# A decoder layer with a retrieval mixer on one core: the residual is kept in the result, and two of the last stores become accumulating DMAs

## The reference

```
    x = x + concat(attn, conv) @ w_out
    h = rms(x) ; q = h @ w_q ; the 16 best of 128*128 experts per head, by two sets of 128 keys
    ug = take(u, experts) ; vg = take(v, experts)              # (tokens, 128, 2048)
    act = gelu(einsum("tkd,td->tk", ug, h)) * gates
    x = x + einsum("tk,tkd->td", act, vg)
```

## Time and profile before

| | us |
|---|---|
| median of 3 runs | 2934.63 (2933.8 to 2936.33) |
| the profiled execution | 2936.09 |
| its span | 2934.0 |

### The profile page before, as it was taken

How to read it: one execution, slowest core, us unless ns; L and a number is a source line. 1 busy time by engine, 2 the same in 40 slices (tenths; PEclk the granted TensorE clock), 3 DMA queues, 4 the chain that set the end, 5 groups by cost and what they waited for, 6 DMA issues and landing times.

```text
span 2934.0 us, 40429 instructions
## 1 busy us (share of the span) xinstructions
PE 2875.9 (98%) x14769; PEld 2544.0 (87%) x14769; DVE 2391.8 (82%) x3106; ACT 1056.5 (36%) x1375; POOL 1667.4 (57%) x1078
## 2 busy tenths in 40 slices
PE   7999999999999999999999999999999999999999
PEld 6888778778899999999999999999997778877787
DVE  6555888855678898988989898899777989999898
ACT  4121333341333343434433343434233333333333
POOL 1000555500116667666766566577868888887762
PEclk9999999999999999999999999999999999999999
DMA  8998999979978998999999999999999999999999
GB/s 297 331 354 276 304 306 298 305 280 330 312 256 304 327 350 307 346 322 345 330 314 348 315 332 331 335 345 365 334 363 387 415 418 417 419 420 418 420 417 375
DMA packets 332718, 1010.00 MB, mean 344 GB/s; under 512 B 65748, under 2 KB 182496, under 8 KB 247072
## 3 DMA queue, kind: packets, MB, share of 16 engines
q1 hardware_dynamic: 181648, 523.28, 47.8%
q0 software_dynamic: 113344, 454.44, 42.7%
q10 hardware_dynamic: 37584, 30.43, 3.2%
HBM read 881.01 MB, written 127.01 MB: 344 GB/s over the span
## 4 chain that ended last, share of the span: by engine, by line
PE 56%; DVE 15%; POOL 10%; issue 8%; DMA 8%; ACT 1%; ACTq 0%; DVEq 0%; SPq 0%; POOLq 0%
PE ps L2021 18%; PE ps L2023 17%; PE ps L2022 17%; POOL dots L975 5%; DMA v_ring<-in_peer_v,experts 3%; DVE x_rows L1871 3%; POOL v_ring L986 3%; DVE u_row L1862 2%; DMA v_two<-in_peer_v 2%; PE ps L2262 2%; DVE x_one L1969 1%; DVE uT_lo L1830 1%; POOL grid L967 1%; DVE uT_lo L1835 1%; DVE v_lo L1920 1%
## 5 line engine op out<-in xcount | busy, mean ns | idle before, releaser
L2021 PE MATMUL ps<-hT_hi,uT_hi 128*128 128x384 f32 x2048 | 697.8, 341 | 6.8 <-DVE uT_lo L1835 2.6
L2023 PE MATMUL ps<-h2T_lo,uT_hi 128*128 128x384 f32 x2048 | 686.1, 335 | 0.0
L2022 PE MATMUL ps<-hT_hi,uT_lo 128*128 128x384 f32 x2048 | 684.9, 334 | 0.0
L967 POOL DMA_INDIRECT grid<-gates,grid_cells x256 | 541.7, 2116 | 80.3 <-issue 80.3
L2021 PE MATMUL ps<-v_hi,a_hi 128*128 128x512 f32 x1024 | 406.5, 397 | 26.0 <-DVE v_lo L1920 25.4
L2022 PE MATMUL ps<-v_hi,a_lo 128*128 128x512 f32 x1024 | 404.0, 395 | 0.0
L2023 PE MATMUL ps<-v_lo,a_hi 128*128 128x512 f32 x1024 | 403.8, 394 | 0.0
L1342 ACT ACTIVATE v_hi<-v_two 128x2048 fp32r<-128x2048 f32 x126 | 241.6, 1919 | 450.0 <-PE ps L2023 387.2
L2021 PEld LDWEIGHTS ps<-hT_hi,uT_hi 128*128 128x128 f32 x2048 | 384.6, 188 | 18.8 <-DVE uT_lo L1835 9.5
L2022 PEld LDWEIGHTS ps<-hT_hi,uT_lo 128*128 128x128 f32 x2048 | 384.9, 188 | 1.9
L2023 PEld LDWEIGHTS ps<-h2T_lo,uT_hi 128*128 128x128 f32 x2048 | 384.3, 188 | 0.0
(11 more groups left out here) (210 smaller groups left out, 4956.7 us busy)
## 6 DMA issues: line engine op xcount, KB each, us to landing
v_two<-in_peer_v SPq DMA_DIRECT2D x63, 2048.0 KB
u_tile<-uT_all SPq DMA_DIRECT2D x70, 1024.0 KB
u_tile<-in_peer_u SPq DMA_DIRECT2D x58, 1024.0 KB
grid_rows<-grid SPq DMA_DIRECT2D x32, 1024.0 KB
half_rows<-in_peer_u SPq DMA_DIRECT2D x58, 512.0 KB, 7.0
uT_all<-half_turned POOLq DMA_DIRECT2D x232, 128.0 KB, 5.0
near_rows<-in_peer_u SPq DMA_DIRECT2D x25, 1024.0 KB, 8.9
uT_all<-near_turned SPq DMA_DIRECT2D x100, 256.0 KB, 7.0
```

The source lines that it names most:

```text
L967: pool.indirect_dma_start(out=grid, out_offset=bass.IndirectOffsetOnAxis(ap=grid_cells[:, d, col:col + 1], axis=0), in_=gates[:, 2 + d, co ...
L2021: mm(out, a_hi, b_hi, start=first, stop=False)
L2022: mm(out, a_lo, b_hi, start=False, stop=False)
L2023: return mm(out, a_hi, b_lo, start=False, stop=last)
```

## The change

1. SP stores the residual of blocks 1 to 3 into the rows of the result itself, not into x_mid, which is gone.
2. x_one isn't loaded. The first of its 128 sums is a product (`tensor_scalar`), the others are as before. Behind the last of them POOL adds x_one onto block 1 of the result with an accumulating DMA (1 MB).
3. x_end for block 2 isn't loaded. DVE copies the four banks of block 2 out of PSUM, and POOL adds them onto block 2 of the result in two halves (512 KB each, behind the second and the fourth copy).
4. Block 3 is as before, with its residual loaded from the result.
5. SP ends behind its own stores and the three of POOL.

```diff
             for t in range(1, TB):
                 sp.wait_ge(out_added[t], OUT_CHUNKS)
-                sp.dma_start(x_mid[t - 1], x_rows[:, t, :]).then_inc(x_mid_stored, 16)
+                sp.dma_start(out_v[t], x_rows[:, t, :]).then_inc(x_mid_stored, 16)
...
             load_group(1, 1)
-            sp.dma_start(x_one[:, :], x_mid[0]).then_inc(x_in[1], 16)
...
-            for d in range(DENSE):
-                sp.dma_start(x_end[d][:, :], x_mid[1 + d]).then_inc(x_in[2 + d], 16)
+            sp.dma_start(x_end[1][:, :], out_v[3]).then_inc(x_in[3], 16)
             sp.dma_start(out_v[0], x_rows[:, 0, :]).then_inc(out_stored, 16)
-            sp.wait_ge(v_used, TILES)
-            sp.dma_start(out_v[1], x_one[:, :]).then_inc(out_stored, 16)
-            for d in range(DENSE):
-                for m in range(TB):
-                    cols = slice(m * CHUNK, (m + 1) * CHUNK)
-                    sp.wait_ge(x_end_ready, TB * d + m + 1)
-                    sp.dma_start(out_v[2 + d][:, cols], x_end[d][:, cols]).then_inc(out_stored, 16)
-            sp.wait_ge(out_stored, 16 * (2 + TB * DENSE))
+            for m in range(TB):
+                cols = slice(m * CHUNK, (m + 1) * CHUNK)
+                sp.wait_ge(x_end_ready, TB + m + 1)
+                sp.dma_start(out_v[3][:, cols], x_end[1][:, cols]).then_inc(out_stored, 16)
+            sp.wait_ge(out_stored, 16 * (1 + TB))
+            sp.wait_ge(sums_stored, 16 * 3)
...
+            pool.wait_ge(x_mid_stored, 16 * SWEPT_BLOCKS)
+            pool.wait_ge(v_used, TILES)
+            pool.dma_start(out_v[1], x_one[:, :], accum_op=ALU.add).then_inc(sums_stored, 16)
+            for half in range(2):
+                cols = slice(half * D // 2, (half + 1) * D // 2)
+                pool.wait_ge(x_end_ready, TB // 2 * (half + 1))
+                pool.dma_start(out_v[2][:, cols], x_end[0][:, cols], accum_op=ALU.add).then_inc(sums_stored, 16)
...
-                if c == 0:
-                    dve.wait_ge(x_in[1], 48)
...
+                if c == 0:
+                    v.tensor_scalar(x_one[:, :], v_ring[0][:, :], acts[:, 0:1], None, ALU.mult).then_inc(v_used, 1)
+                    return
...
-            for d in range(DENSE):
-                dve.wait_ge(x_in[2 + d], 48)
-                for m in range(TB):
-                    cols = slice(m * CHUNK, (m + 1) * CHUNK)
-                    dve.wait_ge(dense_done, TB * d + m + 1)
-                    v.tensor_tensor(x_end[d][:, cols], ps_dense[d][:, cols], x_end[d][:, cols], ALU.add)\
-                        .then_inc(x_end_ready, 1)
+            for m in range(TB):
+                cols = slice(m * CHUNK, (m + 1) * CHUNK)
+                dve.wait_ge(dense_done, m + 1)
+                v.tensor_copy(x_end[0][:, cols], ps_dense[0][:, cols]).then_inc(x_end_ready, 1)
+            dve.wait_ge(x_in[3], 48)
+            for m in range(TB):
+                cols = slice(m * CHUNK, (m + 1) * CHUNK)
+                dve.wait_ge(dense_done, TB + m + 1)
+                v.tensor_tensor(x_end[1][:, cols], ps_dense[1][:, cols], x_end[1][:, cols], ALU.add)\
+                    .then_inc(x_end_ready, 1)
```

More of the change, by code:

```diff
@@ L391, in decoder_layer @@
         mix_all = nc.dram_tensor("mix_all", (KT, P, SEQ), F32, kind="Internal").ap()
-        x_mid = nc.dram_tensor("x_mid", (SWEPT_BLOCKS, P, D), F32, kind="Internal").ap()
         ps = ctx.enter_context(nc.psum_tensor("ps", [P, 8, CHUNK], F32))
@@ L511, in decoder_layer @@
         out_stored = sem("out_stored")
+        sums_stored = sem("sums_stored")
         dve_step = sem("dve_step")
```

## The result

The changed kernel takes 2942.77 us (median of 22 runs, 2936.83 to 2948.88). The kernel before, on the same chip between the same runs, takes 2936.05 us (22 runs, 2933.39 to 2941.9). The ratio is 1.0022 with a 95% interval of 1.0016 to 1.0028, so the change costs 6.5 us (4.7 to 8.2): slower, by 0.22%, just more than the 0.2% that the prediction took for the least that a measurement can tell. The forecast was +3.5 us, no change. The base differs too: the prediction added to the 2934.63 us of three runs, and the median of 22 lies 1.4 us higher. So of the 4.7 us between 2938.1 and 2942.77, 1.4 are the base and 3.3 the effect.

What follows compares the result with a forecast made beforehand. PE (busy 193.15 of 200 us) and the DMA engines (share 1.01) were taken as nearly exhausted together in the last stage. Adding stores at the end +4.0, early gain -0.5: +3.5 us, 2938.1 us, range 2933.0 to 2942.5.

Steps and rivals of the forecast that it cites:

- Stores of blocks 1 to 3 into the result: SP's queue: three transfers of the same size at the same place, to the result instead of x_mid; cost 0.
- Copies and first sum: DVE: block 2's adds become PSUM copies, block 1's first sum a product without x_one as input; cost 0 each.
- The early gain: Start of last stage: without x_one's load v_two lands 2.5 us sooner; mostly handed back later, 0.5 us left.
- POOL's issue: End of kernel: an adding issue takes 1.16 us, starting at 2922.5 when the last sum is done.
- The case in which v_lo holds POOL's issue: DVE's v_lo, 2922.43 to 2924.71, delays POOL's issue: +5.7 us, 2940.3; chance 0.05.
- The rate of the addition: POOL's adding transfers at the end: twice the plain time, 5.0 us per MB, ratio read from small packets.
- The two other rates: Adding transfers at the plain rate, 2.5 us per MB (chance 0.23), or three passes, 7.5 us per MB (chance 0.18).
- the three-pass case: End of kernel: reading source, reading result and writing in turn, 7.5 us per MB; +8.5 us, 2943.1; chance 0.18.
- The work of the whole transfers: DMA engines at the end: 5.0 us for x_one and 5.0 for block 2's halves, then 2.8 for block 3's chunks.
- The begin, and the landing behind the last byte: Tail: first add moves from 2924.0, after the last sum at 2922.5; landing comes 0.8 us behind the last byte.
- The end of the program: Span's end: 0.4 us behind the last landing, as in the kernel before; landed 2937.6, end 2938.0.
- the load's neighbour stall: Sign: PE's stall ahead of the fifth tile near 2214 falls from 3.35 us to under 1 us.

Runs made afterwards that it cites:

- E1: Kernel before without the load of x_one, first sum a product, end as before; ratio to before 0.9996 (0.9987 to 1.0006).
- E5: Kernel before with the load of x_one moved behind the second v_two load on SP's queue; ratio to before 0.9996 (0.9985 to 1.0008).
- E3: Changed kernel with only block 2 added by POOL, block 1 loaded, summed and stored by SP as before; ratio to before 1.0030 (1.0020 to 1.0039).
- E6: Kernel before plus one 8-KB plain store to a scratch tensor as POOL's last act; ratio to before 1.0017 (1.0008 to 1.0026).
- before, again: Kernel before, unchanged, profiled a second time for scatter; stage 721.2 us, tail 11.4 us.
- E4: Changed kernel with POOL's three transfers as plain stores, no adding; ratio to before 1.0003 (0.9993 to 1.0012).
- E8: Changed kernel with x_one added once more, 1 MB onto an unused table, behind the first addition; ratio to before 1.0030 (1.0017 to 1.0042).
- after again: Changed kernel, unedited, profiled a second time for scatter; stage 721.5 us, tail 19.2 us.
- E2: Kernel before with only block 1 changed: x_one not loaded, POOL adds it, block 2 as before; ratio to before 1.0006 (0.9997 to 1.0016).
- E7: Changed kernel with block 2's two POOL transfers plain, block 1 still added; ratio to before 1.0010 (1.0001 to 1.0020).

## Why the prediction was wrong, point by point

**Stores of blocks 1 to 3 into the result: 0. Copies and first sum: 0.** Right. The four copies took 2.79 us, 0.70 each, next to 0.69 for the adds, and they began 3.3 us behind the last sum, as the adds had. DVE's end 8.84 us behind the last sum in both kernels says that neither the missing load of x_end nor the copies moved anything.

**The early gain: 2.5 us at its place, 0.5 left.** The end is right: 0.2 to 0.4 us in the stages, E1 not resolved, E5 handed back within the stage. The size at its place was too high. v_two is ready 1.6 us sooner, not 2.5, and PE's stall in the seven profiles without the load is 1.09 to 2.23 us (mean 1.8), not 0.9. With the load in its old place it is 3.35, 3.49 (E3), 3.24 (E6) and 1.94 (before, again), so the 3.35 of the earlier trace rows was an ordinary value and what was wrong is the 2.5: the time of 1 MB at the full rate was taken off v_two's landing whole. It did no harm, since nearly nothing of it was carried over; the forecast was lucky there.

**POOL's issue.** Its length was nearly right, its start was not: it began 0.6 us behind the last sum, not with it. The adding issue took 1.00 us beside v_lo (2918.28, with v_lo from 2917.61 to 2919.90), where the estimate was 1.16. The plain one of E4 took 0.61. The case in which v_lo holds POOL's issue is excluded. By the Trainium skill (GPSIMD Engine Reference, Specifications), GpSimd contends with VectorE's instructions that have two SBUF inputs. Here v_lo is such an instruction, and the two issues beside it show no hold; a hold is seen in the indirect issues of the earlier trace rows.

**The rate of the addition: twice the plain time.** The ratio holds for single packets in mid-transfer. After, in the 2 us from 2922, with nothing but additions of 8-KB packets in flight, and before, in the 2 us from 2924, with x_one's plain store:
```profile
q0 software_dynamic: 51, 0.42, 100.2%
```
```profile
q1 hardware_dynamic: 108, 0.78, 94.8%
```
51 packets in 1.002 x 2 x 16 = 32.1 engine-us are 629 ns each, at 209 GB/s:
```profile
2922.00:2924.00 2.00, 2.00 (x10) 1.61 (x9) 1.89 (x4) 0.00 (x0) 0.90 (x1) 1.00 1.00 209
```
That is half of the 418 of the earlier trace rows. On before's side 108 packets in 30.3 engine-us are 281 ns each; 13 of them are under 512 bytes (0.78 MB is 95 packets of 8 KB), and the other 95 would be 319 at most. So the ratio is near 2.0. The prediction had read it from packets of 4 bytes, and no row had shown that it would hold for 8 KB. The Trainium skill (Collectives: The Full Stack, The bandwidth ceiling) gives the adding step of a ReduceScatter two reads for each write, and half of AllGather's rate; at this size the trace agrees. The two other rates are excluded, by E8 above all. This deserves a warning: the measured 2942.77 us lies on the time of the three-pass case (2943.1), and a reader of the time alone would take that case for proven. Its 15 us of work for 2 MB are not there; the trace has 11.4 to 11.6.

**The work of the whole transfers: 10.0 us. First wrong term.** Twice the plain rate is right in mid-transfer and too low for the whole. 2 MB took 11.4 to 11.6 us, in after 5.8 for block 1 and 5.6 for block 2. In block 1's MB the first 16 packets, which make all 16 engines busy, take 1.29 us each, 0.66 more than later ones, and that is most of what it has over 5.0. Without such a beginning the price was right: E8's added MB took 5.1. Block 2's MB, in more and smaller packets, took 5.3 in E8, 5.6 and 5.9 in the profiles of after and 6.1 in E3, where the engines were idle before it. Block 3's chunks, with 2.8 us, were right. The sum of work is 14.3 us instead of 12.8: 1.5 us too low. Why the first packets take twice as long is open.

**The begin, and the landing behind the last byte: 1.5 and 0.8 us. Two more wrong sizes.** The data begin to move 2.15 us behind the last sum, not 1.5. The landing was put too high: from the end of the last packet to SP's release it is 0.35 to 0.4 us in both profiles of after. Between the two edges lie 15.5 us in after and 14.6 in after again, with 14.3 and 14.4 us of work in them. The rest, 1.2 and 0.2 us, was in no term: some engines are done before others. The windows of after's last us (columns as in the earlier trace rows) show a few engines still at work when the others have finished:
```profile
2932.00:2933.00 1.00, 0.00 (x0) 0.00 (x0) 0.00 (x0) 0.00 (x0) 0.00 (x0) 0.50 1.07 381
2933.00:2934.00 1.00, 0.00 (x0) 0.00 (x0) 0.00 (x0) 0.00 (x0) 0.00 (x0) 0.50 0.47 176
2934.00:2935.00 1.00, 0.00 (x0) 0.00 (x0) 0.00 (x0) 0.00 (x0) 0.00 (x0) 0.50 0.11 41
2935.00:2936.00 1.00, 0.00 (x0) 0.00 (x0) 0.00 (x0) 0.00 (x0) 0.00 (x0) 0.50 0.02 8
```
In before the share is 0.99 to the end of the stores. What makes single engines late here I could not settle. An addition and plain chunks stand in the same engines, and E8, with the same mixture, has no such thin end.

**The end of the program: 0.4 us behind the last landing. The step that failed.** I took the distance between the last landing and the span's end from before and carried it over to a program whose last transfers are POOL's. The DRAIN of POOL ends 3.1 to 3.2 us behind the landing of its last transfer in after, after again, E2, E4, E7 and E8, and 4.6 us behind it in E6 (2931.5 to 2936.1), and the program waits for it. In the kernel before, POOL's last transfer was a gather issued at 2904.8. Its last packet is at 2919.4 and the DRAIN ends at 2922.7, 3.3 us behind that packet (in after 3.4), so the same closing time stood in the profile of before, 11 us ahead of the end, where it cost nothing. SP's end to the span's end is 1.6 and 2.1 us now: 1.2 and 1.7 us too low. The prediction asked who waits for SP's last wait, but not what POOL itself does when it has nothing left.

The terms together, in us:

| term | predicted | after | after, again |
|---|---|---|---|
| last sum to the first packet | 1.5 | 2.15 | 2.15 |
| work of the engines | 12.8 | 14.3 | 14.4 |
| engines done unevenly | 0 | 1.2 | 0.2 |
| last packet to SP's release | 0.8 | 0.35 | 0.4 |
| SP's release to the span's end | 0.4 | 1.6 | 2.1 |
| tail | 15.5 | 19.6 | 19.2 |

The effect by the profiles, 7.8 to 8.2 less 0.2 to 0.4, is 7.4 to 8.0 us; the timed one is 6.5, with an interval of 4.7 to 8.2 that holds them.

**The cases.** The forecast's mechanism was right, its size too small by 3.0 us. The range, 2933.0 to 2942.5, missed the time by 0.3 us; the base, 1.4 us higher, is more than that. The slower side of the forecast rested nearly all on the case of three passes (0.18 of 0.22), which is excluded. What happened instead was no case: the work (1.5 us), the end of the program (1.2 to 1.7) and the begin (0.65) were all too low, together by 3.4 and 4.0 us in the two profiles. Begin, landing and program end had one number each and no bound. Of the signs named ahead, the load's neighbour stall (under 1 us) failed, the 0.69 us of the copies, the full engines under 400 GB/s and x_one's landing between 5 and 8 us (7.9) held, and the last landing came 9.2 us behind DVE's end (2935.7 less 2926.5; 8.2 in the second profile), not 6 to 7.

No kernel here beats the one before: E1 and E5 are not told apart from it. Adding by another engine's queue, and adding smaller pieces so that block 2 starts earlier, were not tried.

## What to carry to other kernels

A DMA that adds is a transfer of twice the length, and it is cheap only while the DMA engines have a hole: 1 MB that was free 3.3 us ahead of the last copies added 1.2 us to plain stores, 1 MB that came free last added 4. When work moves to another engine's queue at the end of a program, look at how that engine closes, and not only at the semaphore that waits for the data; the profile of before has the closing DRAIN in it, and how far its end lies behind that queue's last packet. And when a term stands behind the last byte, bound it by itself: nothing hides it.

## What the runs showed of the hardware that was not expected

- POOL's closing DRAIN ends 3.1 to 3.2 us behind the landing of its last DMA in six profiles with 1 to 3 MB on its queue, and 4.6 us behind one of 8 KB (landing 2931.5, end 2936.1). Why the small one has more is open. One such store at the end cost 4.6 us of tail, 5.0 us timed (2.4 to 7.6).
- 2.10 MB in the same 432 packets take 5.2 us of the 16 engines plain and 11.4 to 11.6 us adding. In mid-transfer an 8-KB packet takes 629 ns adding.
- The first 16 adding packets of 8 KB took 1.29 us each, the later ones 629 ns. The first MB of additions took 5.8 us, one right behind it 5.1.
- A 1-MB adding issue on POOL takes 1.00 us, a plain one 0.61, both beside a two-input DVE instruction.
